# Values as the stationary operand of the sample attention's products

## The chip, the cores and the metric

The kernel runs on one core of a Trainium2 chip. The metric is the time of one execution on the device in microseconds. Everything is float32 unless a tile is marked fp32r.

## What is computed

The reference is one layer of a hybrid decoder: a recurrent branch (RWKV-7) and a differential attention side by side, an output projection, and then a mixer of product-key experts. It runs on 512 prompt tokens (with 16 learned ones ahead of them) and on 8 sample tokens, one from each of 8 sequences with a past of 1024 tokens. The change concerns the attention of the sample tokens alone:

```
s   = q . k_past * scale - slope(h) * distance      # 4 heads, 2 components each
pr  = softmax(s over the 1024 past tokens and the new one)
att = pr[component 0] - lam * pr[component 1]
o   = att[past] @ v_past + att[new] @ v             # per head: 128 numbers
```

The past keys and values lie in pages of 128 tokens, which a page table names; each sequence has 8 pages. A later step normalises o per head (`head_norm`) and projects it.

## The kernel before

The program is a row of stages. Each stage has one instruction list for each engine, semaphores between them, and ends when all of its engines are done. `attend_sample` is one of them; `attend_prompt` comes before it and `head_norm` behind it. Both attentions leave their result in `oT`, which holds it transposed: 128 value channels on the partitions, then head, then token. The sample tokens are its last 8 columns.

`attend_sample` first spreads the 8 queries over all partitions (L1202) and prepares constants. Then it goes through the 8 sequences, in a software pipeline that `sequences` writes out: the first sequence alone, a hardware loop over pairs, and the last one. K and V have two buffers each. SP's queue loads the pages of K, GpSimd's queue those of V and the new token's value row `vn`. Each load waits until its buffer is free: K's on VectorE (`kfree`), V's on ScalarE (`vfree`).

For one sequence the work goes from engine to engine. VectorE multiplies K by the query (`product`, L1322) and sums over the 64 channels (`reduce`, L1328). TensorE turns the scores of 8 pages into rows (`turn`, L1214). ScalarE copies them (`lay`), VectorE finds the maximum (`maximum`), ScalarE takes exponents (`exponent`), and VectorE makes the factors of the two components (`scale`). TensorE merges the components and turns the weights back to one token per partition (`combine`, L1221 and L1222), and ScalarE copies them into `at` and `atn` (`weights`). At last TensorE forms the products with the values (`values`, L1231 and L1232), and ScalarE copies the result out and frees the V buffer (`keep`, L1278). TensorE's order in the loop is combine of the sequence before, turn of this one, values of the one before.

In `values` the attention weights are the stationary side: for each page a block of 128 tokens x 4 heads is loaded, and all 512 columns of the page's values (4 heads x 128 channels) move past it:

```
for pg in range(NPAGE):
    nc.tensor.matmul(pO[:, :], at[:, pg, :], V[b][:, pg, :], start=(pg == 0), stop=False)
nc.tensor.matmul(pO[:, :], atn[:, :], vn[b][:, :], start=False, stop=True).then_inc(summed, 1)
```

The result is a tile of 4 x 512 in which row h and columns 128h to 128h+127 are head h's output; the other blocks (one head's weights with another head's values) are not used. `keep` copies the whole tile into a part of Q's memory (`orow`). When all 8 sequences are through, TensorE gathers: 32 small products (L1248) pick each head's row and turn it into a column, and VectorE copies the 32 columns into `oT` (L1368).

Of the kernel before, what the change touches and what calls it, by code (L numbers as in the profile page):

```python
# [18 lines left out]
ACT = mybir.ActivationFunctionType  # L19
AX = mybir.AxisListType  # L20

P = 128
D = 1024
KD = D // P
META, SEQ, DEC = 16, 512, 8
NP_ = META + SEQ
T = NP_ + DEC
TQ = SEQ + DEC
# [13 lines left out]
HA, DV = 4, 128  # L42
PAGE, NPAGE, PAST = 128, 8, 1024
# [69 lines left out]
def sc(nc):  # L113
    return nc.scalar.activation
# [1009 lines left out]
def attend_sample(nc, c, proj, oT, past, vnew):  # L1124
# [4 lines left out]
    with Stage(nc, "dec") as s:  # L1129
        K, V, vn, pages = (past[n] for n in ("K", "V", "vn", "pages"))  # L1130
        Q = s.sb("Q", [P, DEC, 512])
# [7 lines left out]
        st = s.sb("st", [HC, 3])  # L1139
        at = s.sb("at", [P, NPAGE, HA])  # L1140
        atn = s.sb("atn", [1, HA])
        orow = Q[0:HA, :, :]
        pQ = [s.ps(f"pQ{b}", [P, 512]) for b in range(2)]
        pN = s.ps("pN", [P, 512])
        pR = s.ps("pR", [HC, PAST])
        pA = s.ps("pA", [P, 16 * NPAGE, HA])[:, 0:NPAGE, :]
        pA1 = s.ps("pA1", [1, 512])
        pO = s.ps("pO", [HA, 512])
        names = ("taken", "step", "pstep", "prods", "newd", "newc", "qrep", "qcop", "sdone", "turned", "laid",
                 "maxed", "expd", "combd", "backt", "bcop", "summed", "kept", "gathered", "dstep", "astep")  # L1150
        (taken, step, pstep, prods, newd, newc, qrep, qcop, sdone, turned, laid,
         maxed, expd, combd, backt, bcop, summed, kept, gathered, dstep, astep) = (s.sem(n) for n in names)
        kin, vin, kfree, vfree = ([s.sem(f"{n}{b}") for b in range(2)] for n in ("kin", "vin", "kfree", "vfree"))
        blk = s.block()

# [2 lines left out]
        def sequences(eng, first, middle, last):  # L1158
            first(0, 0)
            with eng.Fori(0, DEC // 2 - 1) as i:  # L1160
                middle(i, 1)
                middle(i, 2)
            middle(DEC // 2 - 1, 1)
            last(DEC // 2 - 1, 1)

        @blk.sync
        def _(sp):
            for b in range(2):
                sp.sem_inc(kin[b], 16 * NPAGE)
            with sp.Fori(1, DEC // 2) as i:  # L1170
                for b in range(2):
                    sp.wait_ge(kfree[b], i)
                    load_pages(sp, past["ck"], pages, i * (2 * NPAGE) + b * NPAGE, K[b], kin[b])
# [19 lines left out]
        @blk.tensor  # L1193
        def _(pe):
            for b in range(2):
                pe.sem_inc(vfree[b], 1)
            for b in range(DEC):
                if b >= 2:
                    pe.wait_ge(qcop, b - 1)
                for h in range(HA):  # L1200
                    q = proj[:, 14 + h, zs + b:zs + b + 1].to_broadcast([P, P])
                    last = nc.tensor.matmul(pQ[b % 2][:, h * P:(h + 1) * P], q, c["ident"][:, :], start=True, stop=True)  # L1202
                last.then_inc(qrep, 1)
            pe.wait_ge(prods, 1)
            for b in range(DEC):
                last = nc.tensor.matmul(pN[0:HC, b:b + 1], qk[:, b, :, :].rearrange("p e h -> p (e h)"), c["ones"][:, 0:1],
                                        start=True, stop=True)
            last.then_inc(newd, 1)

            def turn(i, off):  # L1210

                pe.wait_ge(sdone, i * 2 + (off + 1))
                for pg in range(NPAGE):
                    last = nc.tensor.transpose(pR[:, pg * P:(pg + 1) * P], Sc[:, pg, :, :].rearrange("p e h -> p (e h)"), c["ident"][:, :])  # L1214
                last.then_inc(turned, 1)

            def combine(i, off):

                pe.wait_ge(combd, i * 2 + (off + 1))
                for pg in range(NPAGE):  # L1220
                    nc.tensor.matmul(pA[:, pg, :], rows[:, pg * P:(pg + 1) * P], comb[:, :], start=True, stop=True)  # L1221
                nc.tensor.matmul(pA1[:, 0:HA], rows[:, PAST:PAST + 1], comb[:, :], start=True, stop=True).then_inc(backt, 1)  # L1222

            def values(i, off):

                b = off % 2
                pe.wait_ge(bcop, i * 2 + (off + 1))
                pe.wait_ge(kept, i * 2 + (off + 1))
                pe.wait_ge(vin[b], (i + (off // 2 + 1)) * (16 * (NPAGE + 1)))
                for pg in range(NPAGE):  # L1230
                    nc.tensor.matmul(pO[:, :], at[:, pg, :], V[b][:, pg, :], start=(pg == 0), stop=False)  # L1231
                nc.tensor.matmul(pO[:, :], atn[:, :], vn[b][:, :], start=False, stop=True).then_inc(summed, 1)  # L1232

            def middle(i, off):
                combine(i, off - 1)
                turn(i, off)
                values(i, off - 1)

            def last_one(i, off):
                combine(i, off)  # L1240
                values(i, off)

            pe.sem_inc(kept, 1)
            sequences(pe, turn, middle, last_one)
            pe.wait_ge(kept, DEC + 1)
            for b in range(DEC):
                for h in range(HA):
                    last = nc.tensor.matmul(pN[:, h * DEC + b:h * DEC + b + 1], orow[:, b, h * DV:(h + 1) * DV],  # L1248
                                            c["ident"][0:HA, h:h + 1], start=True, stop=True)
            last.then_inc(gathered, 1)  # L1250

        @blk.scalar
        def _(act):
            for b in range(DEC):
                act.wait_ge(qrep, b + 1)
                sc(nc)(Q[:, b, :], pQ[b % 2][:, :], ACT.Copy).then_inc(qcop, 1)
            act.wait_ge(newc, 1)

            def lay(i, off):

                act.wait_ge(turned, i * 2 + (off + 1))
                sc(nc)(rows[:, 0:PAST], pR[:, :], ACT.Copy).then_inc(laid, 1)
                sc(nc)(rows[:, PAST:PAST + 1], new[:, bass.ds(i * 2 + off, 1)], ACT.Copy).then_inc(laid, 1)

            def exponent(i, off):
                act.wait_ge(maxed, i * 2 + (off + 1))
                sc(nc)(rows[:, :], rows[:, :], ACT.Exp, bias=st[:, 0:1], accum_out=st[:, 1:2]).then_inc(expd, 1)

            def weights(i, off):
                act.wait_ge(backt, i * 2 + (off + 1))  # L1270
                sc(nc)(at[:, :, :], pA[:, :, :], ACT.Copy).then_inc(astep, 1)
                act.wait_ge(astep, i * 2 + (off + 1))
                sc(nc)(atn[:, :], pA1[:, 0:HA], ACT.Copy).then_inc(bcop, 1)

            def keep(i, off):
                b = off % 2
                act.wait_ge(summed, i * 2 + (off + 1))
                sc(nc)(orow[:, bass.ds(i * 2 + off, 1), :], pO[:, :].unsqueeze(1), ACT.Copy).then_inc(kept, 1)  # L1278
                act.sem_inc(vfree[b], 1)

            def first(i, off):
                lay(i, off)
                exponent(i, off)

            def middle(i, off):
                weights(i, off - 1)
                lay(i, off)
                exponent(i, off)
                keep(i, off - 1)

            def last_one(i, off):
                weights(i, off)
                keep(i, off)

            sequences(act, first, middle, last_one)

        @blk.vector
        def _(dve):
# [65 lines left out]
                scale(i, off, 2 + 3 + 1)  # L1364

            sequences(dve, first, middle, last_one)
            dve.wait_ge(gathered, 1)
            nc.vector.tensor_copy(oT[:, :, SEQ:TQ], pN[:, 0:HA * DEC].rearrange("p (h b) -> p h b", h=HA)).then_inc(taken, 1)  # L1368


def head_norm(nc, c, oT):
# [856 lines left out]
```

## Time and profile before

| | |
|---|---|
| median of three runs | 2864.57 us (2863.24 to 2865.25) |
| the profiled execution's own time | 2869.91 us |
| its span, first to last instruction | 2868.5 us |
| mean granted TensorE clock | 0.885 |
| TensorE busy | 2319.0 us, 81% |
| VectorE busy | 1836.4 us, 64% |
| GpSimd busy | 1085.3 us, 38% |
| ScalarE busy | 774.3 us, 27% |

In the profile PE is TensorE's matmuls and PEld its weight loads, DVE is VectorE, ACT is ScalarE, POOL is GpSimd, SP is SyncE. A row of the timeline begins with its start in us from the span's start and its length in us, then engine, line, operation, the output tile, an arrow and the inputs, the shapes (of a matmul: the stationary block, then the moving one) and the number of instructions that the row merges; in brackets stands the idle time ahead of it and what ended that. A row for a stretch of time has the stretch, its length, and then the busy time of PE, PEld, DVE, ACT and POOL (or only of those asked for) with the number of records that touch the stretch; its last three columns are the granted TensorE clock as a share of full speed, the busy share of the DMA engines, and GB/s. The clock has two levels: 1.00 is 2.4 GHz, 0.50 is 1.2 GHz.

### The profile page before, as it was taken

The numbers are of one execution on the slowest core, as the hardware profiler recorded it, in microseconds if no ns is written. First come the engines' busy times: TensorE is split into PE (matmuls) and PEld (weight loads), VectorE is DVE, ScalarE is ACT, GpSimd is POOL, SyncE is SP. The second block draws the span as 40 slices with busy tenths as digits, with TensorE's granted clock in tenths as the row PEclk, the third lists the DMA queues.
The fourth block names the chain that finished last, engine by engine and source line by source line (L and its number), as shares of the span: only waits on it lengthen the run. The fifth ranks groups of instructions, "written<-read, shape, count | busy, mean of one in ns | idle before, by whom it ended". The sixth has DMA issues, their size and how long they took to land. (4 is left out here: it accounts for less than half of the span.)

```text
span 2868.5 us, 48299 instructions
## 1 busy us (share of the span) xinstructions
PE 2319.0 (81%) x17079; PEld 2113.6 (74%) x17079; DVE 1836.4 (64%) x3685; ACT 774.3 (27%) x1387; POOL 1085.3 (38%) x1003
## 2 busy tenths in 40 slices
PE   3974888268696977890078399999999999999998
PEld 3973787135434977780066399999999999999998
DVE  3127555575663132599899267777777777777776
ACT  1112000113221222110099332333323333233331
POOL 2420000000131422032389355555555555555552
PEclk8985988685686989995599699999999999999999
DMA  2310000112471212220018976666766667666761
GB/s 62 88 46 8 3 3 3 36 60 59 151 259 37 80 59 59 61 58 0 0 49 192 226 276 250 243 246 251 263 250 242 218 245 262 243 243 239 254 249 50
DMA packets 232151, 403.55 MB, mean 141 GB/s; under 512 B 45590, under 2 KB 166865, under 8 KB 215410
## 3 DMA queue, kind: packets, MB, share of 16 engines
q1 hardware_dynamic: 189809, 251.21, 27.1%
q0 software_dynamic: 42240, 151.03, 15.5%
q8 instruction: 58, 0.95, 0.1%
q14 instruction: 44, 0.35, 0.0%
HBM read 370.81 MB, written 31.39 MB: 140 GB/s over the span
## 5 line engine op out<-in xcount | busy, mean ns | idle before, releaser
L2005 DVE TENSOR_TENSOR experts_G<-experts_G,experts_M 128x392 f32<-128x392 f32 x128 | 198.7, 1552 | 296.0 <-ACT experts_G L1922 292.0
L1877 PE MATMUL experts_pV<-experts_GH,experts_VH 128*128 128x392 f32 x1024 | 369.9, 361 | 0.0
L1866 PE MATMUL experts_pH<-keep_xh,experts_UH 128*128 128x392 f32 x1024 | 350.9, 343 | 0.0
L1866 PE MATMUL experts_pH<-keep_xl,experts_UH 128*128 128x392 f32 x1024 | 349.2, 341 | 0.0
L1866 PE MATMUL experts_pH<-keep_xh,experts_UL 128*128 128x392 f32 x1024 | 348.5, 340 | 0.0
L1877 PE MATMUL experts_pV<-experts_GH,experts_VL 128*128 128x392 f32 x1024 | 348.2, 340 | 0.0
L1877 PE MATMUL experts_pV<-experts_GL,experts_VH 128*128 128x392 f32 x1024 | 347.4, 339 | 0.0
L1970 POOL TENSOR_TENSOR experts_VL<-experts_V,experts_VH 128x2048 fp32r<-128x2048 f32 x64 | 294.7, 4605 | 128.3 <-ACT experts_VH L1916 127.3
L2009 DVE TENSOR_TENSOR keep_xT<-experts_pV,keep_xT 128x392 f32<-128x392 f32 x512 | 264.5, 551 | 6.2 <-PE experts_pV L1877 6.2
L1910 ACT ACTIVATE experts_UH<-experts_pU 128x512 fp32r<-128x512 f32 x256 | 151.7, 593 | 217.5 <-PE experts_pU L1856 217.5
L1877 PEld LDWEIGHTS experts_pV<-experts_GL,experts_VH 128*128 128x128 f32 x1024 | 193.3, 189 | 0.0
L1866 PEld LDWEIGHTS experts_pH<-keep_xh,experts_UL 128*128 128x128 f32 x1024 | 193.0, 188 | 0.0
L1866 PEld LDWEIGHTS experts_pH<-keep_xh,experts_UH 128*128 128x128 f32 x1024 | 192.8, 188 | 0.0
L1877 PEld LDWEIGHTS experts_pV<-experts_GH,experts_VH 128*128 128x128 f32 x1024 | 192.7, 188 | 0.0
L1866 PEld LDWEIGHTS experts_pH<-keep_xl,experts_UH 128*128 128x128 f32 x1024 | 192.7, 188 | 0.0
L1877 PEld LDWEIGHTS experts_pV<-experts_GH,experts_VL 128*128 128x128 f32 x1024 | 192.4, 188 | 0.0
L1922 ACT ACTIVATE experts_G<-experts_pH 128x392 f32<-128x392 f32 x128 | 63.6, 497 | 465.1 <-PE experts_pH L1866 465.1
L1999 DVE TENSOR_TENSOR experts_UL<-experts_pU,experts_UH 128x512 fp32r<-128x512 f32 x256 | 173.6, 679 | 9.2 <-ACT experts_UH L1910 9.2
L1030 POOL IOTA att_dist<- 128x528 f32 x1 | 0.6, 571 | 460.0 <-POOLq L73 460.0
L1856 PE MATMUL experts_pU<-keep_ident,experts_U 128*128 128x128 f32 x1024 | 155.1, 275 | 13.7 <-DMA experts_U<-in_peer_u 7.9
L1966 POOL TENSOR_TENSOR experts_GL<-experts_G,experts_GH 128x392 fp32r<-128x392 f32 x128 | 151.5, 1205 | 0.0
L1692 PE MATMUL spread_pm<-spread_B,spread_A 128*128 128x128 f32 x784 | 124.2, 296 | 32.1 <-POOL spread_A L1739 27.3
(420 smaller groups left out, 4997.6 us busy)
## 6 DMA issues: line engine op xcount, KB each, us to landing
experts_U<-in_peer_u SPq DMA_DIRECT2D x64, 1024.0 KB
experts_V<-in_peer_v SPq DMA_DIRECT2D x64, 1024.0 KB, 5.2
experts_M<-scratch_gates SPq DMA_DIRECT2D x64, 392.0 KB, 3.3
keep_K<-in_cache_k SPq DMA_DIRECT2D x64, 256.0 KB, 3.4
keep_V<-in_cache_v POOLq DMA_DIRECT2D x64, 256.0 KB, 3.9
inp_w<-in_w_in SPq DMA_DIRECT2D x22, 512.0 KB, 3.8
scratch_gates<-spread_M SPq DMA_DIRECT2D x1, 8704.0 KB, 35.6
gate_w<-in_w_in SPq DMA_DIRECT2D x16, 512.0 KB, 3.8
```

The costliest lines, as they stand in the source:

```text
L1030: nc.gpsimd.iota(dist[:, :], pattern=[[-1, WM]], base=META + 3 * P, channel_multiplier=1, allow_small_or_imprecise_dtypes=True).then_inc(b ...
L1692: last = nc.tensor.matmul(pm[g][:, t, :], A[g][:, t, :], B[g][:, t, :], start=True, stop=True)
L1856: last = nc.tensor.transpose(pU[a][:, k, :], U[q.b][:, e, (4 * a + k) * P:(4 * a + k + 1) * P], c["ident"][:, :])
L1866: last = nc.tensor.matmul(pH[e][:, 0:DT], u[e][:, k, :], x[:, k, :], start=(k == 0 and n == 0), stop=(k == KD - 1 and n == 2))
L1877: last = nc.tensor.matmul(pV[n % 4][:, 0:DT], l, r, start=(t == 0), stop=(t == 5))
L1910: sc(nc)(UH[e][:, 4 * a:4 * a + 4, :], pU[a][:, :, :], ACT.Copy).then_inc(u_hi, 1)
L1922: sc(nc)(G[e][:, :], pH[e][:, 0:DT], ACT.Gelu).then_inc(gelued, 1)
L1966: nc.gpsimd.tensor_tensor(GL[q.b][:, e, :], G[e][:, :], GH[q.b][:, e, :].bitcast(F32), ALU.subtract).then_inc(g_lo, 1)
L1970: nc.gpsimd.tensor_tensor(VL[q.b][:, :, :], V[q.b][:, :, :], VH[q.b][:, :, :].bitcast(F32), ALU.subtract).then_inc(v_lo, 1)
L1999: nc.vector.tensor_tensor(UL[e][:, 4 * a:4 * a + 4, :], pU[a][:, :, :], UH[e][:, 4 * a:4 * a + 4, :].bitcast(F32), ALU.subtract).then_inc( ...
L2005: nc.vector.tensor_tensor(G[e][:, :], G[e][:, :], M[q.b][:, e, :], ALU.mult).then_inc(gated, 1)
L2009: nc.vector.tensor_tensor(acc[:, n, 0:DT], pV[n % 4][:, 0:DT], acc[:, n, 0:DT], ALU.add).then_inc(added, 1)
```

## The change

In `values` the two sides trade places. V's block of one page and one head (128 tokens x 128 channels) is now stationary, and that head's one column of the attention weights moves. Four heads are gone through one after the other, and each sums its 8 pages and the new token into its own column of `pO`. So the result is 128 channels x 4 heads, as `oT` has it. `keep` copies these four columns straight into `oT`. The gather at the end, VectorE's copy and the semaphores of both are gone.

```diff
-        orow = Q[0:HA, :, :]
...
-        pO = s.ps("pO", [HA, 512])
+        pO = s.ps("pO", [P, 512])
...
                 pe.wait_ge(vin[b], (i + (off // 2 + 1)) * (16 * (NPAGE + 1)))
-                for pg in range(NPAGE):
-                    nc.tensor.matmul(pO[:, :], at[:, pg, :], V[b][:, pg, :], start=(pg == 0), stop=False)
-                nc.tensor.matmul(pO[:, :], atn[:, :], vn[b][:, :], start=False, stop=True).then_inc(summed, 1)
+                for h in range(HA):
+                    own = slice(h * DV, (h + 1) * DV)
+                    for pg in range(NPAGE):
+                        nc.tensor.matmul(pO[:, h:h + 1], V[b][:, pg, own], at[:, pg, h:h + 1], start=(pg == 0), stop=False)
+                    last = nc.tensor.matmul(pO[:, h:h + 1], vn[b][:, own], atn[:, h:h + 1], start=False, stop=True)
+                last.then_inc(summed, 1)
...
             sequences(pe, turn, middle, last_one)
-            pe.wait_ge(kept, DEC + 1)
-            for b in range(DEC):
-                for h in range(HA):
-                    last = nc.tensor.matmul(pN[:, h * DEC + b:h * DEC + b + 1], orow[:, b, h * DV:(h + 1) * DV],
-                                            c["ident"][0:HA, h:h + 1], start=True, stop=True)
-            last.then_inc(gathered, 1)
...
                 act.wait_ge(summed, i * 2 + (off + 1))
-                sc(nc)(orow[:, bass.ds(i * 2 + off, 1), :], pO[:, :].unsqueeze(1), ACT.Copy).then_inc(kept, 1)
+                sc(nc)(oT[:, :, bass.ds(i * 2 + (SEQ + off), 1)], pO[:, 0:HA].unsqueeze(2), ACT.Copy).then_inc(kept, 1)
                 act.sem_inc(vfree[b], 1)
...
             sequences(dve, first, middle, last_one)
-            dve.wait_ge(gathered, 1)
-            nc.vector.tensor_copy(oT[:, :, SEQ:TQ], pN[:, 0:HA * DEC].rearrange("p (h b) -> p h b", h=HA)).then_inc(taken, 1)
```

## Rows read from the trace of the kernel before

**Rows 1.** Busy time by engine, from the first values to the next stage.
```profile
771.40:868.01 96.61, 93.38 (x319) 30.10 (x318) 60.76 (x39) 23.04 (x49) 28.92 (x54) 0.88 0.70 231
868.01:882.18 14.17, 12.98 (x64) 12.90 (x64) 0.19 (x1) 0.59 (x2) 0.00 (x0) 0.56 0.00 0
```

**Rows 2.** Timeline of TensorE's matmuls, 765 to 792 us.
```profile
765.98 3.57 PE L1221 MATMUL dec_pA<-dec_comb,dec_rows 8*128 8x4 f32 x16 [8.46 <-DVE dec_comb L1345]
769.48 0.19 PE L1222 MATMUL dec_pA<-dec_comb,dec_rows 8*1 8x4 f32 x2
769.60 1.87 PE L1214 MATMUL dec_pR<-keep_ident,dec_Sc 128*8 128x128 f32 x8
771.40 8.31 PE L1231 MATMUL dec_pO<-keep_V,dec_at 128*4 128x512 f32 x16
...
780.59 1.94 PE L1221 MATMUL dec_pA<-dec_comb,dec_rows 8*128 8x4 f32 x16
...
783.55 7.03 PE L1231 MATMUL dec_pO<-keep_V,dec_at 128*4 128x512 f32 x16
790.51 1.02 PE L1232 MATMUL dec_pO<-keep_vn,dec_atn 1*4 1x512 f32 x2
791.46 1.94 PE L1221 MATMUL dec_pA<-dec_comb,dec_rows 8*128 8x4 f32 x16
```

**Rows 3.** Groups of instructions by line, 740 to 900 us: count, busy us, mean ns.
```profile
L1322 DVE TENSOR_TENSOR keep_K<-keep_K,dec_Q 128x4096 f32<-128x4096 f32 x8 | 35.4, 4425 | 11.5 <-DMA keep_K<-in_cache_k 10.5 <-issue 0.8
L1328 DVE TENSOR_REDUCE dec_Sc<-keep_K 128x64 f32<-128x4096 f32 x8 | 35.2, 4401 | 0.0
```

**Rows 4.** Timeline of all engines, 857 to 883 us.
```profile
857.41 0.19 PE L1222 MATMUL dec_pA<-dec_comb,dec_rows 8*1 8x4 f32 x2
...
858.31 8.72 PE L1231 MATMUL dec_pO<-keep_V,dec_at 128*4 128x512 f32 x16 [0.71 <-DMA keep_vn<-scratch_v]
...
868.01 0.59 ACT L1278 ACTIVATE dec_Q<-dec_pO 4x512 f32<-4x512 f32 x1 [9.99 <-PE dec_pO L1232]
...
868.65 12.98 PE L1248 MATMUL dec_pN<-keep_ident,dec_Q 4*128 4x1 f32 x64 [0.68 <-ACT dec_Q L1278]
881.67 0.19 DVE L1368 COPY keep_oT<-dec_pN 128x32 f32<-128x32 f32 x1 [29.88 <-PE dec_pN L1248]
882.18 2.21 ACT L1384 ACTIVATE subln_sq<-keep_oT 128x520 f32<-128x520 f32 x4 [13.58 <-PEq L73]
```

**Rows 5.** TensorE alone in stretches of L1221 and L1248, with the granted clock.
```profile
765.98:769.48 3.50, 3.50 (x16) 0.50 0.72 175
780.59:782.47 1.88, 1.88 (x18) 1.00 0.79 154
...
868.65:869.75 1.10, 1.10 (x9) 0.93 0.00 0
...
870.85:881.63 10.78, 10.78 (x51) 0.50 0.00 0
```

**Rows 6.** The prompt attention: value products on TensorE's timeline; one stretch's clock.
```profile
654.73 1.52 PE L1064 MATMUL att_pO<-att_AT,keep_v_tok 128*128 128x128 f32 x4 [0.51 <-ACT att_AT L1087]
...
670.35 2.80 PE L1064 MATMUL att_pO<-att_AT,keep_v_tok 128*128 128x128 f32 x10 [0.83 <-ACT att_AT L1087]
...
690.00:735.00 45.00, 37.66 (x129) 23.93 (x128) 23.40 (x59) 16.16 (x54) 0.00 (x0) 0.50 0.00 0
```

**Rows 7.** Timeline: the first keep, and the values that wait for V.
```profile
780.79 0.59 ACT L1278 ACTIVATE dec_Q<-dec_pO 4x512 f32 x1 [5.66 <-PE dec_pO L1232]
...
796.81 8.39 PE L1231 MATMUL dec_pO<-keep_V,dec_at 128*4 128x512 f32 x14 [2.33 <-DMA keep_vn<-scratch_v]
```

**Rows 8.** L1202's records (PE, PEld) in a stretch, with the granted clock.
```profile
741.10:742.20 1.10, 1.10 (x12) 1.10 (x11) 1.00 0.92 194
```

**Rows 9.** Single records of two lines: ns at least, median and most.
```profile
L1231 PE MATMUL dec_pO<-keep_V,dec_at x128: 589/592/1061, 771.4 to 866.4; 128*4 128x512 f32 x128
L1248 PE MATMUL dec_pN<-keep_ident,dec_Q x64: 245/347/348, 868.7 to 881.3; 4*128 4x1 f32 x64
```

More of the change, by code:

```diff
@@ L1147, in attend_sample @@
         pA1 = s.ps("pA1", [1, 512])
-        pO = s.ps("pO", [HA, 512])
[L1149 to L1152, printed above, removed]
+        pO = s.ps("pO", [P, 512])
+        names = ("step", "pstep", "prods", "newd", "newc", "qrep", "qcop", "sdone", "turned", "laid",
+                 "maxed", "expd", "combd", "backt", "bcop", "summed", "kept", "dstep", "astep")
+        (step, pstep, prods, newd, newc, qrep, qcop, sdone, turned, laid,
+         maxed, expd, combd, backt, bcop, summed, kept, dstep, astep) = (s.sem(n) for n in names)
         kin, vin, kfree, vfree = ([s.sem(f"{n}{b}") for b in range(2)] for n in ("kin", "vin", "kfree", "vfree"))
```

## The prediction

> **What bounds the kernel now.** I read the summary page first: TensorE is busy for 81% of the span, but that is an average over many stages, so what the change is worth has to be read in the stage that it edits. I then asked for the busy time of each engine in the stretch of the sample attention. Its value products begin at 771.40 us and the last of them is done at 868.01 us, 96.61 us later. TensorE is busy for 93.38 us of that, VectorE for 60.76, GpSimd for 28.92 and ScalarE for 23.04 [rows 1]. TensorE sets the pace. Then come 14.17 us up to the next stage, which are the end of this one: 12.98 us of TensorE and next to nothing elsewhere [rows 1].
>
> TensorE's timeline shows what it does for each of the eight samples: combine (L1221, L1222), turn (L1214), values (L1231, L1232), and again, back to back [rows 2]. Where nothing disturbs it, one round takes 10.87 us, from 780.59 to 791.46, and the values are 7.91 of that (783.55 to 791.46). VectorE's two large operations are 4.43 + 4.40 us per sample [rows 3], so even with its small operations it fits beside such a round. The timeline of the end shows the gather as one chain: the last row copied at 868.01, the gather's 64 records from 868.65, VectorE's copy at 881.67, and the next stage's first operation at 882.18 [rows 4]. No other engine has work there.
>
> **What the change takes away.** The gather L1248, VectorE's copy, and the handover to each of them. Today the last keep starts at 868.01 and the next stage at 882.18. Afterwards the last keep writes oT itself. It has 4 elements per partition where it had 512; VectorE's copy of 32 elements took 0.19 us and the old keep 0.59 [rows 4], which bound it, and I take 0.2, near the small one. The step to the next stage stays, 882.18 less the copy's end at 881.86, so 0.3 us. That makes 0.5 us in place of 14.17: **13.7 us gone**, all of it on the path. The other seven keeps also get shorter, but they lie beside TensorE's next combine, so I count nothing for them. If that cover went, they would be worth 0.4 us each. The wider pO and the two semaphores fewer issue nothing on a path that I can see: nothing.
>
> **What it adds.** Each product L1231 now appears as four, with a 128x128 block of V as the stationary side and one moving column. In the trace each product of f32 is two records (8 pages, 16 records [rows 2]). So values becomes 4 x 9 x 2 = 72 records of a 128-column weight load and a one-column product, where it was 18 records of a 4-column load and 512 moving columns.
>
> The trace has such records. L1221 loads 128 columns and moves 4, and L1248 loads 128 and moves 1. In L1248's stretch the weight loads cover 12.90 of TensorE's 12.98 us [rows 1]. At the full clock of 2.4 GHz sixteen records of L1221 took 780.59 to 782.47, 0.1175 us each [rows 2, 5]. At a granted clock of 0.50, which is 1.2 GHz, they took 765.98 to 769.48, 0.219 each [rows 2, 5]; and of L1248's records 51 touch a stretch of 10.78 us, one of which began before it, 0.216 each [rows 5]. Those blocks have 4 or 8 partitions. For 128 there is the prompt attention, whose value products already have 128x128 stationary blocks: from 4 records to 10 its group grew from 1.52 to 2.80 us, 0.213 each, at 0.50 [rows 6]. The number of partitions doesn't show. I take 0.216, between 0.213 and 0.219.
>
> So values costs 72 x 0.1175 = 8.46 us at the full clock against 7.91 today, nearly even; at 1.2 GHz it costs 72 x 0.216 = 15.55. The clock decides this change.
>
> **Which clock it gets.** The gather answers it. TensorE came into it at the full clock. In its first 1.10 us the granted clock averaged 0.93; a microsecond later it was 0.50, and it stayed there for the remaining 10.78 us, although TensorE's rows cover all of that time [rows 5]. Under this stream, weight loads without a pause and one column moved, the clock did not hold. It is not a matter of few partitions alone: in the prompt attention, with 128-partition blocks and TensorE covered for 37.66 of 45 us, the clock was also 0.50 throughout [rows 6]. Today it rose during L1231: the combine ahead of the first values group has 0.50, the one behind it 1.00 [rows 2, 5]. These products are gone after the change, and records like the gather's stand in their place; of the rest of a round, combine is of the same kind and turn is short (1.80 us at 1.2 GHz). So I take 1.2 GHz for the whole stage. That slows combine and turn too.
>
> The Trainium skill has a rule against this. The page "TensorE: Matmul & The Clock Gate", section "Why this matters for your kernels", lays mid-kernel drops of the clock to idle gaps between bursts; a stream with no gap should then stay at the full clock. The gather's rows disagree: the clock fell inside a stream without gaps. By that rule this change would come out as the first rival below.
>
> **The sum at 1.2 GHz.** Between two values groups, with the clock at 1.2 GHz, TensorE needs 3.62 us for combine (765.98 to 769.60) and 1.80 for turn and the copied weights (769.60 to 771.40), 5.42 together [rows 2]. There are six such gaps. The seventh has no turn: 3.50 for L1221 and about 0.9 from L1222 to the values (857.41 to 858.31) [rows 4], so 4.4. Eight values groups are 124.4; the gaps are 32.5 + 4.4; the last record's tail is about 0.15. That is 161.5 us in place of 96.61: **64.9 us more**. With the 13.7 gone, the change costs **51.2 us**. Against the profiled execution's 2869.91 us that gives 2921.1. The three runs shown have a median of 2864.57, 5.3 below it, so I forecast 2915.8, say 2916.
>
> Who waits for the longer values: behind them on TensorE stand the next combine and turn, behind these ScalarE's weights and rows, and VectorE's maximum. All of them are shorter than a round of 21 us. V's buffers come free later, but a load from free to landed took 15.4 us (keep's end 781.38 to 796.81) [rows 7], and a buffer would now have 15.55 + 2 x 5.42 = 26.4. TensorE's wait for V, 2.33 us at its longest [rows 7], would go; it is inside the 96.61. K's loads on SP's queue start on VectorE's word, once per round, and have 21 us as well.
>
> **Rivals.**
> 1. *The clock stays at 2.4 GHz* (the other sign). Place: the values groups; it decides if loading full 128-partition blocks keeps the clock, which the gather, with 4, doesn't show. Then V binds: a buffer needs 15.4 us to load, 8.5 to be used and 0.2 to be freed, 24.1 per two samples. With the second values group at about 784.5, the eighth ends at 784.5 + 3 x 24.1 + 8.5 = 865.3, so the stage takes 93.9 us, 2.7 less; with the 13.7 it is -16. The waits for V cost TensorE the full clock at times: today a group that starts at 1.2 GHz takes 9.19 us (771.40 to 780.59), 1.3 more, and three such groups give 4 back [rows 2]. That makes -12, about 2853. Against it: the prompt attention at 0.50 with 128 partitions.
> 2. *The clock goes back and forth.* L1214 with its 128 moving columns lifts it at times; L1202, which spreads the sample queries (128 columns loaded, 128 moved), reached 1.00 [rows 8]. Half the time at each level lies midway between +51 and -12: +20, about 2884. Against it: L1214 is 8 records in a round of 94.
> 3. *Products that add into one column don't overlap.* Then a record costs its full 0.347 us, the median length of L1248's products [rows 9], and not 0.216: 576 x 0.131 = 75 more, 2991. Against it: L1231's sixteen records add into one place today, and at the full clock they start 0.435 us apart (783.55 to 790.51, over 16) [rows 2], though each lasts 0.59 [rows 9].
>
> **How the numbers follow.** Chances: 1.2 GHz throughout 0.74, rival 1 0.12, rival 2 0.10, rival 3 0.04. In the likeliest case alone the records' bounds (0.213 to 0.219) are only 2 us either way; the first record group or a turn at the full clock, or a wait that I don't see, is worth some 10, so its own range is 2903 to 2926. The range reaches over rival 2: 2870 to 2930; rivals 1 and 3 are left out. About 0.2% (5.7 us) is what a measurement of this kernel can tell from no change. Faster by more than that is rival 1: 0.12. Within it is the edge between rivals 1 and 2: 0.02. Slower: 0.86.
>
> **What would show it.** After the change the granted clock between 771 us and the stage's end should be 0.50, with values groups near 15.5 us, combines near 3.6 and turns near 1.8, and the first ACTIVATE of the next stage half a microsecond after the last keep starts. L1248 is gone and TensorE has no wait for V. A granted clock near 1.00 in the values groups, or record steps far from 0.216 us at 0.50, would make the prediction wrong.

## The result, and the profile after

The changed kernel takes 2922.2 us (median of four runs, 2918.83 to 2925.02), the kernel before 2864.9 (four runs beside them). The ratio is 1.020, with a 95% interval of 1.0183 to 1.0218: slower by 57.3 us, where 51 were forecast. The profiled execution took 2918.83 us, 48.9 more than the one of before; that one was, as the prediction says, 5 us above its median, and this one is 3 us below its own.

First the stage by stretches, in the profile after: from the first values group to the last keep, from there to the next stage, and one values group and the combine and turn behind it. The columns are those of [rows 1].

```profile
768.84:931.49 162.65, 162.14 (x751) 157.29 (x750) 60.83 (x39) 20.20 (x49) 29.01 (x54) 0.50 0.47 138
931.49:931.97 0.48, 0.00 (x0) 0.00 (x0) 0.00 (x0) 0.18 (x2) 0.00 (x0) 0.50 0.00 0
...
768.84:784.67 15.83, 15.83 (x73) 15.72 (x73) 11.44 (x7) 2.35 (x4) 0.00 (x0) 0.50 0.61 180
784.67:789.93 5.26, 5.26 (x27) 4.63 (x28) 0.00 (x0) 0.54 (x3) 1.64 (x3) 0.50 0.77 208
```

The last three columns begin with the granted clock. It was 0.88 on average in the 96.61 us of [rows 1] and is 0.50 for all of the 162.65 now, although TensorE's rows leave out only half a microsecond. Weight loads (the second sum) went from 30.10 us to 157.29; VectorE and GpSimd did the same work as before, and ScalarE 2.8 us less, as keep copies 4 elements per partition and no longer 512. The 14.17 us at the end became 0.48.

TensorE's timeline after, one round; it answers to [rows 2].

```profile
784.67 3.55 PE L1220 MATMUL dec_pA<-dec_comb,dec_rows 8*128 8x4 f32 x16
...
788.27 1.87 PE L1213 MATMUL dec_pR<-keep_ident,dec_Sc 128*8 128x128 f32 x8
789.93 3.41 PE L1232 MATMUL dec_pO<-dec_at,keep_V 128*128 128x1 f32 x16
793.27 0.58 PE L1233 MATMUL dec_pO<-dec_atn,keep_vn 1*128 1x1 f32 x2
793.78 3.58 PE L1232 MATMUL dec_pO<-dec_at,keep_V 128*128 128x1 f32 x16
797.29 0.58 PE L1233 MATMUL dec_pO<-dec_atn,keep_vn 1*128 1x1 f32 x2
...
805.76 3.55 PE L1220 MATMUL dec_pA<-dec_comb,dec_rows 8*128 8x4 f32 x16
```

A round is 21.09 us (784.67 to 805.76) with no idle time in it: none of these rows has a bracket. A head's 16 records take 3.51 us (793.78 to 797.29), 0.219 each, and the two of the new token 0.50. The end of the stage, all engines, answers to [rows 4]:

```profile
930.88 0.58 PE L1233 MATMUL dec_pO<-dec_atn,keep_vn 1*128 1x1 f32 x2
931.49 0.18 ACT L1274 ACTIVATE keep_oT<-dec_pO 128x4 f32<-128x4 f32 x1 [16.21 <-PE dec_pO L1233]
931.97 2.21 ACT L1378 ACTIVATE subln_sq<-keep_oT 128x520 f32<-128x520 f32 x4 [0.30 <-PEq L73]
```

### The profile page after: what moved, and what is told of

Same layout as the page of the kernel before. It is cut to its first block and busy times, and to the rows that moved or that the text cites. A ratio compares the mean times of both kernels' runs of the same rounds, so it can differ in the third digit from the quotient of the medians.

```text
span 2917.4 us, 49032 instructions
## 1 busy us (share of the span) xinstructions
PE 2372.8 (81%) x17447; PEld 2226.0 (76%) x17447; DVE 1835.6 (63%) x3684; ACT 771.9 (26%) x1387; POOL 1086.8 (37%) x1003
## 5 line engine op out<-in xcount | busy, mean ns | idle before, releaser
L1850 PE MATMUL experts_pU<-keep_ident,experts_U 128*128 128x128 f32 x1024 | 154.7, 275 | 12.9 <-DMA experts_U<-in_peer_u 8.3
```

Of the source, the lines that this page charges most:

```text
L1850: last = nc.tensor.transpose(pU[a][:, k, :], U[q.b][:, e, (4 * a + k) * P:(4 * a + k + 1) * P], c["ident"][:, :])
```

## The experiments

The theory ahead of them: a stream of weight loads that moves one column loses the clock, and the clock is the whole price.

**The same loads, 128 columns moved.** Each weight column is read 128 times over, so that the moving side is as wide as the stationary block. All of it lands in the one bank of `pO`, and keep takes one column of each head.

```diff
-nc.tensor.matmul(pO[:, h:h + 1], V[b][:, pg, own], at[:, pg, h:h + 1], start=(pg == 0), stop=False)
+nc.tensor.matmul(pO[:, h * P:h * P + 128], V[b][:, pg, own], at[:, pg, h:h + 1].to_broadcast([P, 128]), start=(pg == 0), stop=False)
...
-sc(nc)(oT[...], pO[:, 0:HA].unsqueeze(2), ACT.Copy)
+sc(nc)(oT[...], pO[:, :].rearrange("p (h x) -> p h x", h=HA)[:, :, 0:1], ACT.Copy)
```

> The change, but each weight column is repeated so that 128 columns move past each block of V (one bank per sample is filled, one column per head is kept). The same 72 weight loads per sample. Theory (a stream of weight loads with one moved column loses the clock, and the clock is the whole price): the granted clock in the values groups returns to about 1.00, a record takes 0.11 to 0.12 us as in L1202, values falls from 15.8 to about 8.5 us, the stage from 162.7 to 94 to 99 us, and the kernel takes 10 to 16 us less than the one before the change (ratio 0.994 to 0.997). Rival (128-partition blocks as the stationary side hold the engine at 1.2 GHz whatever moves): clock 0.50, values 15.8 us, ratio 1.02.

Measured: 2867.7 us (11 runs) against 2863.3, ratio 1.0018 (1.0009 to 1.0027): 4.5 us more than the kernel before, where I expected 10 to 16 less. But TensorE multiplies 128 times as many columns as in the change, and the kernel is some 50 us faster than the change. In its profile, a combine with its turn, one values group, and the whole stage:

```profile
785.92:789.16 3.24, 3.24 (x28) 2.79 (x27) 2.02 (x1) 0.54 (x3) 0.93 (x2) 0.85 0.84 226
789.16:799.72 10.56, 10.56 (x74) 9.71 (x74) 8.31 (x6) 2.35 (x4) 3.89 (x8) 0.88 0.96 317
775.24:882.19 106.95, 106.43 (x751) 96.01 (x750) 61.17 (x39) 20.25 (x49) 28.92 (x54) 0.88 0.67 209
```

The clock came back, so the rival (128-partition blocks hold it at 1.2 GHz) is out. But the stage is 107 us and not the 94 to 99 that I expected. The clock is not 1.00 all the time, and TensorE's timeline shows where it is lost: of four heads with the same 18 records, the first one is the long one in this round, as in the next four.

```profile
785.92 1.84 PE L1220 MATMUL dec_pA<-dec_comb,dec_rows 8*128 8x4 f32 x16
...
787.81 1.55 PE L1213 MATMUL dec_pR<-keep_ident,dec_Sc 128*8 128x128 f32 x8
789.16 3.11 PE L1232 MATMUL dec_pO<-dec_at,keep_V 128*128 128x128 f32 x16
...
792.62 2.05 PE L1232 MATMUL dec_pO<-dec_at,keep_V 128*128 128x128 f32 x16
...
795.01 2.05 PE L1232 MATMUL dec_pO<-dec_at,keep_V 128*128 128x128 f32 x16
```

Something in combine or turn lowers the clock (the turn of this round took 1.55 us, against 1.04 at the full clock), and it comes back only in the values. At the full clock a record takes 0.124 us (1.98 for 16, 792.62 to 794.60), and the pair of the new token 0.41: 9.6 us a group, 1.1 more than I had priced.

**32 columns moved.** The same edit with 32 in place of 128.

> The change with 32 moved columns per block instead of 1. By the theory the weight loads still set the length of a record, so the time shows the clock alone: 1.02 of the kernel before with 0.50 granted, or 0.995 with 1.00. I lean to 0.50, as the moving columns would cover only a quarter of a record. The rival (stationary blocks alone) expects 0.50 and 1.02 as well, so this run only bounds how much has to move.

Measured: 2925.2 us (4 runs), ratio 1.0219 (1.0202 to 1.0235). The first values group:

```profile
771.02:787.20 16.18, 16.18 (x73) 15.73 (x73) 11.51 (x7) 2.35 (x4) 0.00 (x0) 0.50 0.58 177
```

With 32 columns the clock was 0.50 and the time that of the change.

**The gather with 128 columns.** If moved columns alone decide, the kernel before can be helped the same way.

```diff
-nc.tensor.matmul(pN[:, n:n + 1], orow[:, b, h * DV:(h + 1) * DV], c["ident"][0:HA, h:h + 1], start=True, stop=True)
+nc.tensor.matmul(pN[:, n:n + P], orow[:, b, h * DV:(h + 1) * DV], c["ident"][0:HA, h:h + 1].to_broadcast([HA, P]), start=True, stop=True)
```

(n counts the columns h * DEC + b in rising order, so that each product writes over the surplus of the one ahead of it.)

> The kernel before the change; only its gather moves 128 repeated columns per product where it moved one (blocks of 4 partitions, the same 64 weight loads). Theory: the clock stays up and the gather takes 64 x 0.1175 = 7.5 us in place of 13.0, so the kernel is about 5.5 us faster (ratio 0.998). Rival (blocks of few partitions lose the clock whatever moves): 13 us or more and ratio 1.000 or above.

Measured: 2864.6 us (11 runs), ratio 1.0005 (0.9996 to 1.0014), no difference. TensorE alone in the gather, from its start on, granted clock after the counts:

```profile
867.41:868.51 1.10, 1.10 (x9) 1.00 0.00 0
868.51:870.50 1.99, 1.99 (x20) 1.00 0.00 0
871.00:878.48 7.48, 7.48 (x36) 0.50 0.00 0
```

The clock fell in a gather that moves 128 columns. So the theory, as I had it, was wrong: columns are not all. These blocks have 4 partitions. The gather took 11.07 us and not 7.5.

**No gather.** It prices the removed part alone. The sample columns of `oT` are set to a constant, so the sample attention's result is left out.

```diff
-            pe.wait_ge(kept, DEC + 1)
-            ... (the 32 products of L1248)
-            dve.wait_ge(gathered, 1)
-            nc.vector.tensor_copy(oT[:, :, SEQ:TQ], pN[:, 0:HA * DEC].rearrange("p (h b) -> p h b", h=HA)).then_inc(taken, 1)
+            nc.vector.memset(oT[:, :, SEQ:TQ], 1.0).then_inc(taken, 1)
```

> The kernel before the change without its gather; the sample columns of the result are set to a constant, so the sample attention's output is left out. It prices the removed part alone: theory 13.3 us less (ratio 0.9953), with the next stage beginning half a microsecond after the last keep ends. Rival (the next stage waits for something else there): less than 10 us.

Measured: 2853.2 us (6 runs) against 2863.3, ratio 0.9963 (0.9950 to 0.9975), 10 us less. In its profile the next stage begins 0.89 us after the last keep's start, in place of 14.17:

```profile
863.76 0.59 ACT L1272 ACTIVATE dec_Q<-dec_pO 4x512 f32<-4x512 f32 x1 [9.76 <-PE dec_pO L1232]
864.65 1.69 ACT L1377 ACTIVATE subln_sq<-keep_oT 128x520 f32<-128x520 f32 x3 [0.30 <-PEq L73]
```

By that step 13.3 us go; the expected ratio, 0.9953, lies inside the interval. The removed part is real. Its values code is that of before, and from 769.77 to 863.76 it took 93.99 us; in three further profiles with that code it took 94.07 to 94.28. The 96.61 of the profile before was 2.5 us above these.

**The gather with 128 partitions.** Q's memory holds the queries on the other 124 partitions, and the moving side has zeros there. So the same result comes from blocks of 128 partitions, with 128 columns moved or with one. The edit with 128 is shown against the experiment with 4 partitions and 128 columns.

```diff
-nc.tensor.matmul(pN[:, n:n + P], orow[:, b, h * DV:(h + 1) * DV], c["ident"][0:HA, h:h + 1].to_broadcast([HA, P]), start=True, stop=True)
+nc.tensor.matmul(pN[:, n:n + P], Q[:, b, h * DV:(h + 1) * DV], c["ident"][:, h:h + 1].to_broadcast([P, P]), start=True, stop=True)
```

> The kernel before the change; its gather takes blocks of all 128 partitions (the other 124 meet a zero in the moving side) and moves 128 repeated columns. The theory of moved columns alone fell with the gather of 4 partitions and 128 columns, which lost the clock 3 us in. Second theory: it takes both, many partitions and many moved columns. Then the granted clock stays at 1.00 through the gather, which takes 64 x 0.1175 to 0.124 = 7.5 to 7.9 us in place of 13.0, and the kernel is 5 us faster (ratio 0.998). Rival (a gather at the end of the stage loses the clock for another reason): clock 0.50 from 3 us on, about 11 us, ratio 1.000.

> The kernel before the change; its gather takes blocks of all 128 partitions and moves one column, as the changed values do. Second theory (both are needed): the clock falls as in the gather of before, 13 us. Rival (partitions alone decide): clock 1.00 and 7.5 us.

In the profile with 128 partitions and 128 columns, TensorE alone over the whole gather:

```profile
864.69:872.10 7.41, 7.41 (x64) 1.00 0.00 0
```

With 128 partitions and one column, two stretches of the gather, which took 10.65 us:

```profile
871.63:872.13 0.50, 0.50 (x7) 1.00 0.00 0
...
873.13:873.63 0.50, 0.50 (x4) 0.50 0.00 0
```

With the gathers of before and of the experiment ahead, that is every pairing of 4 or 128 partitions with 1 or 128 columns, all with 64 records in the same place. Three of the four lost the clock on the way (12.98, 11.07 and 10.65 us); the one with both at 128 kept it and took 7.41. The last experiment has that gather too, and there it took 7.41 us again. The three that fell differ in the moment of the fall (1, 3.3 and 3.5 us in), and one profile each doesn't tell if that is more than chance. The 5.6 us are plain in the trace, but the times do not establish them: 2860.5 us (11 runs) against 2863.9, ratio 0.9995 (0.9986 to 1.0004), which reaches over no change. The kernel with 128 partitions and one column has a single run, 2864.0.

**Combine widened too.** To the kernel that moves 128 columns this adds a wide combine: `rows` and `comb` get 128 partitions (zeros from the ninth on), and comb's 4 columns are read 32 times over.

```diff
-nc.tensor.matmul(pA[:, pg, :], rows[:, pg * P:(pg + 1) * P], comb[:, :], start=True, stop=True)
+nc.tensor.matmul(pA[:, pg:pg + P // HA, :], rows[:, pg * P:(pg + 1) * P], comb[:, :].unsqueeze(1).to_broadcast([P, P // HA, HA]), start=True, stop=True)
```

> The change with 128 moved columns per block, and combine widened too: its blocks of 8 partitions become 128 (the rest zeros) and its 4 moved columns become 128 (repeated, later products write over the surplus). Second theory: combine no longer lowers the clock, so all values groups run at 1.00; a round takes 9.6 + 2.9 = 12.5 us in place of 13.8, the stage 97 us, and the kernel about 10 us less than the one before the change (ratio 0.9965). Rival (the turn, with blocks of 8 columns, or the waits lower the clock): rounds stay at 13.8 and the ratio at 1.002.

Measured: 2855.3 us (7 runs) against 2863.9, ratio 0.9969 (0.9957 to 0.9980): 8.5 us faster than the kernel before, and some 66 us faster than the change. A combine with its turn, a values group, and the whole stage:

```profile
778.67:781.64 2.97, 2.97 (x27) 2.65 (x27) 2.97 (x1) 0.54 (x3) 0.75 (x2) 1.00 0.74 235
781.64:791.12 9.48, 9.48 (x74) 8.52 (x72) 6.80 (x7) 2.35 (x4) 4.07 (x8) 1.00 1.00 346
769.19:865.70 96.51, 96.03 (x752) 86.14 (x750) 60.86 (x39) 20.18 (x49) 28.93 (x54) 1.00 0.71 233
```

The granted clock is 1.00 over the whole stage, a round is 12.45 us as expected, and the stage 96.5. So it was the combine (blocks of 8 partitions, 4 columns moved) that lowered the clock in the experiment with 128 columns; the turn, which is unchanged, does not do it alone. The last round shows it without a turn: in both kernels the last values group starts 0.48 us after the combine. First with the narrow combine, the two heads behind it, then with the wide one, the first head:

```profile
869.36 3.14 PE L1232 MATMUL dec_pO<-dec_at,keep_V 128*128 128x128 f32 x16 [0.48 <-ACT dec_atn L1269]
...
873.15 3.78 PE L1232 MATMUL dec_pO<-dec_at,keep_V 128*128 128x128 f32 x16
...
856.07 2.05 PE L1232 MATMUL dec_pO<-dec_at,keep_V 128*128 128x128 f32 x16 [0.48 <-ACT dec_atn L1269]
```

Whether the partitions or the columns matter at combine was not tried apart.

**The kernel before with both widened parts** (the wide combine, and the gather with 128 partitions and columns).

> The kernel before the change with both widened parts: combine and gather with 128 partitions and 128 moved columns. Second theory: the falls of the clock at combine go, so the stage from the first values to the last keep takes 88 to 92 us where 94 to 97 were measured, and the gather 7.5 to 7.9; together 8 to 12 us less (ratio 0.996 to 0.997). Rival (the falls come from the waits for V): 94 us or more and only the gather's 5 us.

Measured: 2859.7 us (11 runs), ratio 0.9987 (0.9978 to 0.9996), 4 us less. In its profile the stage up to the last keep:

```profile
769.49:863.10 93.61, 88.46 (x319) 31.46 (x318) 60.78 (x39) 23.06 (x50) 28.93 (x54) 0.95 0.71 240
```

Here the expectation failed: the clock rose to 0.95 and TensorE has 88.46 us of work where the kernel without the gather had 92.49, but the stage is 93.6 and not 88 to 92. The list of waits says what took the place:

```profile
PE dec_pA L1221 <- DVE dec_comb L1348: 3.6, 2, 1.8
PE dec_pO L1231 <- DMA keep_vn<-scratch_v: 1.1, 1, 1.1
```

The columns are us in total, times, and the longest. TensorE now waits for VectorE's factors at combine, which the kernel without the gather doesn't. Behind two such waits the clock fell, although the combine is wide: 16 records took 3.08 and 3.78 us there, against 2.05 at the full clock.

```profile
802.28 3.08 PE L1221 MATMUL dec_pA<-dec_comb,dec_rows 128*128 128x128 f32 x16 [1.71 <-DVE dec_comb L1348]
...
827.69 3.78 PE L1221 MATMUL dec_pA<-dec_comb,dec_rows 128*128 128x128 f32 x16 [1.85 <-DVE dec_comb L1348]
```

So what the clock gave there went into waits, and the rival was right in part: a wait came ahead of the falls that were left, though it was the wait for VectorE. The 4 us are near the gather's 5.6; the runs do not separate them further.

## Why the prediction was right

**The clock.** The step that decided, 1.2 GHz for the whole stage, is what the trace shows. The rule of the Trainium skill, page "TensorE: Matmul & The Clock Gate", section "Why this matters for your kernels", that idle gaps between bursts cost the clock, would have given rival 1. It does not describe this stage: 162.14 of 162.65 us are covered and the clock is 0.50. Rival 1's own point, that full 128-partition blocks might keep the clock, was not excluded by the gather of before, which has 4 partitions; the change's own profile excludes it, and so does the gather with 128 partitions and one column. My reading of the gather, which named the one moved column, was half of it: 128 moved columns with 4 partitions fell too. And my second ground, the prompt attention at 0.50 [rows 6], pointed the right way by luck: its value products move 128 columns past 128 partitions, and that pairing kept 1.00 in the gather. Its stretch has idle time (37.66 of 45 us are covered) and other shapes between these products; what holds it at 0.50 no run here shows.

**The sizes.** A values group was put at 15.55 us and is 15.83: the records of a page take the upper bound, 0.219 us, and the new token's pair 0.50 and not 0.43. The gap between groups was put at 5.42 and is 5.26. The stage was put at 161.5 and is 162.65; the end at 0.5, and is 0.48. In the two profiles that is 66.0 more and 13.7 less, 52.4 us, where I had 51.2. (A full round has 98 records of TensorE, 72, 18 and 8, and not the 94 that I set against rival 2; it changes nothing there.)

**What is left.** The medians differ by 57.3 us. Of the 4.9 us beyond 52.4, about 2.5 are the long stage in the profile that I started from (96.61 against 94.0 to 94.3 in four others). The other 2 to 3 us no profile places. They are within what the stages ahead vary by: the first values group of the profiles with the code of before starts anywhere from 769.8 to 774.4 us. The same spread hides where the 128-column version's time went: by its trace (12.9 us more than 94.1, 13.7 less) it should be even with the kernel before, and it is 4.5 us slower. In its one profile the first values group starts later than in any other, at 775.24 us, but one profile does not explain a median. That stays open.

**The other rivals.** The turn did not lift the clock (rival 2): it is 0.50 over the whole stage. Products that add into one column overlap (rival 3): a record steps by 0.219 us and lasts 0.352 in the median.

```profile
L1232 PE MATMUL dec_pO<-dec_at,keep_V x512: 212/352/373, 768.8 to 930.6; 128*128 128x1 f32 x171
```

TensorE's waits for V went, as forecast. VectorE's maximum now waits for the turn through ScalarE, 66.9 us in all where it was 8.7, and costs nothing there.

## What to carry to other kernels

Swapping the sides of a product keeps its result and changes what the engine spends its time on. Here 18 records with 512 moved columns became 72 with one, somewhat dearer at 2.4 GHz (8.5 us a group, an estimate from combine's records, against 7.9; 9.6 was measured with 128 columns moved) and twice as dear at the 1.2 GHz that they got. So price such a change at both clocks from records of the same kind, then look what the clock did in the trace's nearest stream. Where TensorE's rows cover all the time and the granted clock is still 0.50, widening the moving side to the width of the block, with copies that nobody reads, brought most of the time back here, where a quarter of that width did nothing; and to hold the full clock, combine ahead of the stream had to be widened with it.

## What the runs showed of the hardware that I had not expected

TensorE's granted clock fell in streams without a gap. In the same place and with the same 64 weight loads it fell with blocks of 4 partitions and 128 moved columns, and with 128 partitions and one column; with 128 of both it stayed at 1.00 (7.41 us against 11.07 and 10.65). And more work was faster: repeating the moved column 128 times, and filling the combine's blocks with zeros and repeating its columns, took the stage from 162.65 to 96.51 us.
